# A two-layer encoder trunk on one core: order and waits in the odd layer's attention and output projection, in its router, and one step of the even layer

## The reference, cut to what matters

```
layer 0: h = x @ w_in -> heads A (sliding window, sinks, ALiBi) and B (forgetting attention)
         x = LN(ALPHA * x + concat(A, B) @ w_out);  x = LN(ALPHA * x + swiglu(x))
layer 1: h = x @ w_in -> q, k in two maps, v;  a = softmax(map 0) - lam * softmax(map 1)
         o = RMSNorm(a @ v) per head;              x = LN(ALPHA * x + o @ w_out)
         router: logits = x @ w_router, top 2 of 8, softmax gates
         x = LN(ALPHA * x + sum over the chosen experts of gate * swiglu_e(x))
```

## Time and profile before

| | us |
|---|---|
| median of 3 runs | 1427.79 |
| lowest, highest | 1424.65, 1428.18 |
| the profiled execution's own time | 1426.34 |
| its span, first to last instruction | 1424.6 |
| PE busy in the span | 1394.3 |
| DVE, ACT busy | 1126.4, 955.9 |
| mean granted clock of TensorE | 0.994 |

### The profile page before, as it was taken

How to read it: one execution, slowest core, us unless ns; L and a number is a source line. 1 busy time by engine, 2 the same in 40 slices (tenths; PEclk the granted TensorE clock), 3 DMA queues, 4 the chain that set the end, 5 groups by cost and what they waited for, 6 DMA issues and landing times.

```text
span 1424.6 us, 19267 instructions
## 1 busy us (share of the span) xinstructions
PE 1394.3 (98%) x7210; PEld 1182.1 (83%) x7210; DVE 1126.4 (79%) x1007; ACT 955.9 (67%) x880; POOL 36.8 (3%) x50
## 2 busy tenths in 40 slices
PE   8999999999999999999999999999999999999996
PEld 8998888889988888888888888888888888888874
DVE  4637655575567888888888888888888888889997
ACT  4655544545654777777777777777777777778774
POOL 1200000000001000000000000000000000000200
PEclk9999999999999999999999999999999999999998
DMA  9825555545146999999999999999999999999950
GB/s 365 324 81 207 203 182 186 198 148 178 60 179 253 424 422 421 412 391 375 366 383 379 375 399 374 372 390 385 374 365 386 382 372 401 376 377 366 384 248 31
DMA packets 64643, 444.85 MB, mean 312 GB/s; under 512 B 7416, under 2 KB 7440, under 8 KB 13008
## 3 DMA queue, kind: packets, MB, share of 16 engines
q1 hardware_dynamic: 59904, 425.75, 76.9%
q0 software_dynamic: 4544, 18.14, 3.5%
q10 hardware_dynamic: 144, 0.27, 0.1%
HBM read 431.54 MB, written 12.59 MB: 312 GB/s over the span
## 4 chain that ended last, share of the span: by engine, by line
PE 93%; DVE 4%; ACT 2%; DMA 1%; issue 0%; SPq 0%; DVEq 0%; ACTq 0%
PE ps L527 26%; PE ps L529 26%; PE ps L528 26%; PE ps L586 6%; PE ps L587 3%; PE ps L909 2%; DVE wlo L1292 1%; PE ps L647 1%; PE ps L699 1%; DMA raw<-w_dense 1%; ACT whi L1002 1%; PE ps L534 0%; PE ps L674 0%; PE ps L867 0%; PE ps L556 0%
## 5 line engine op out<-in xcount | busy, mean ns | idle before, releaser
L1292 DVE TENSOR_TENSOR wlo<-raw,whi 128x2048 fp32r<-128x2048 f32 x398 | 910.0, 2291 | 190.5 <-ACT whi L1002 189.4
L1002 ACT ACTIVATE whi<-raw 128x2048 fp32r<-128x2048 f32 x398 | 762.2, 1918 | 226.6 <-PE ps L529 224.5
L527 PE MATMUL ps<-whi,xt 128*128 128x512 f32 (+1 forms) x1144 | 442.1, 386 | 5.0 <-DVE wlo L1472 2.0
L529 PE MATMUL ps<-whi,xt 128*128 128x512 f32 (+1 forms) x1144 | 435.2, 380 | 0.0
L528 PE MATMUL ps<-wlo,xt 128*128 128x512 f32 (+1 forms) x1144 | 434.7, 380 | 0.0
L527 PEld LDWEIGHTS ps<-whi,xt 128*128 128x128 f32 x1144 | 216.1, 189 | 48.6 <-DVE wlo L1292 5.6
L529 PEld LDWEIGHTS ps<-whi,xt 128*128 128x128 f32 x1144 | 215.9, 189 | 41.1
L528 PEld LDWEIGHTS ps<-wlo,xt 128*128 128x128 f32 x1144 | 216.4, 189 | 38.2
L527 PE MATMUL ps<-whi,hth 128*128 128x512 f32 x464 | 181.8, 392 | 0.5 <-DVE wlo L1292 0.5
L529 PE MATMUL ps<-whi,htl 128*128 128x512 f32 x464 | 181.0, 390 | 0.0
L528 PE MATMUL ps<-wlo,hth 128*128 128x512 f32 x464 | 180.8, 390 | 0.0
(11 more groups left out here) (246 smaller groups left out, 843.9 us busy)
## 6 DMA issues: line engine op xcount, KB each, us to landing
raw<-w_moe SPq DMA_DIRECT2D x336, 1024.0 KB, 7.0
raw<-w_dense SPq DMA_DIRECT2D x62, 1024.0 KB, 4.8
x_slots<-hth POOLq DMA_DIRECT2D x16, 256.0 KB, 10.7
raw<-vec_rows POOLq DMA_DIRECT2D x4, 1024.0 KB, 7.2
y_rows<-work SPq DMA_DIRECT2D x8, 512.0 KB, 7.9
biasb<-x_slots POOLq DMA_DIRECT2D x7, 512.0 KB, 7.9
x<-x_in SPq DMA_DIRECT2D x2, 512.0 KB, 5.2
raw<-w_dense SPq DMA_DIRECT2D x2, 512.0 KB, 10.2
```

The costliest lines, as they stand in the source:

```text
L527: mm(o, lh, rh, start=start, stop=False)
L529: return mm(o, ll, rh, start=False, stop=stop)
L1002: A(unit(whi, j), raw[:, slot * UNIT:(slot + 1) * UNIT], ACT.Copy).then_inc(hi_rdy, 1)
L1292: dve.tensor_tensor(unit(wlo, j), raw[:, slot * UNIT:(slot + 1) * UNIT], unit(whi, j).bitcast(F32), ALU.subtract).then_inc(lo_rdy, 1)
```

## The change

It does the following.

- Layer 0: DVE's 16 bias instructions stand ahead of the split of unit 8 and no longer behind it.
- Turns go through the token tiles of one half of the heads before the other half. Values wait for the first half's copies, and for the rest only ahead of head 4.
- Layer 1: the scores of group 7 stand ahead of the turn of group 6 on PE and DVE; ACT keeps its order. Values 6 no longer wait for the last projection unit's copy at their start but ahead of head 6.
- The table load for the square root goes one unit earlier on ACT. Two warm-up matmuls ahead of `turn(4)` go away. The output projection starts after the first of the two tiles; unit 2 for block 1 is cut in halves around unit 3 for block 0.
- Router: positions of block 0 are taken inside block 1's logits, DVE makes block 0's one-hot at once, and PE gathers block 0's part of three of the four PSUM parts before it waits for block 1's choice. Two banks are cleared by matmuls with zeros. The warm-ups are 8, 4, 3, 8 for 8, 8, 4, 3, 8. On DVE the slot rows and a split stand behind the gather's subtractions.

The diff, cut to its core (new semaphores and the removed copies of blocks that only moved are left out):

```diff
-WARM_START, WARM_FIRST, WARM_NORM, WARM_HEADS = 9, 7, 12, 2
-WARM_ROUTE = (8, 8, 4, 3, 8)
+WARM_START, WARM_FIRST, WARM_NORM = 9, 7, 12
+WARM_ROUTE = (8, 4, 3, 8)
...
+        def part_bank(q):
+            return ps[(2, 3, 0, 1)[q]]
...
                 return i % 2, i // 2, (6, 7, 0, 1)[i]
+            if t == 5:
+                return i // 2, i % 2, i % 2
...
                    {4: [("scores", 4, 4)], 5: [("scores", 5, 0)], 8: [("scores", 6, 8)],
-                    9: [("turn", 6, 0), ("scores", 7, 0)],
-                    11: [("values", 6, 12), ("turn", 7, 0)]}]
+                    9: [("scores", 7, 0), ("turn", 6, 0)],
+                    11: [("values", 6, 11), ("turn", 7, 0)]}]
...
                         keep_warm(WARM_NORM, 3)
-                    if j == 0 and t == 4:
-                        keep_warm(WARM_HEADS, 4)
...
                 n = TR_BEFORE[g]
-                for kt in range(GROUPS[g][1] + 1):
-                    for half in range(2):
+                for half in range(2):
+                    for kt in range(GROUPS[g][1] + 1):
...
                         for i in range(4):
-                            r = pe.transpose(ps[prob_banks(g)[half]][:, i * P:(i + 1) * P],
+                            r = pe.transpose(ps[prob_banks(g)[n % 2]][:, i * P:(i + 1) * P],
...
                 kind, qblk, _ = GROUPS[g]
-                pe.wait_ge(pt_ev, TR_BEFORE[g + 1])
+                pe.wait_ge(pt_ev, TR_BEFORE[g] + qblk + 1)
...
                 for h in range(8):
+                    if h == 4:
+                        pe.wait_ge(pt_ev, TR_BEFORE[g + 1])
+                    if (g, h) == (6, 6):
+                        pe.wait_ge(in_ev, U_IN_E + U_IN_O)
...
-            def mix(k, tb, first, last, lh, ll):
+            def mix(k, tb, first, last, lh, ll, parts=range(4)):
                 h, l = as_rows(whi, k), as_rows(wlo, k)
-                for i in range(4):
+                for i in parts:
...
                         r.then_inc(y_left, 1)
-                if tb == 1:
+                if tb == 1 and parts[-1] == 3:
...
-            def out_rows(k0, u, tb):
+            def out_rows(k0, u, tb, parts=range(4)):
...
                     lambda r2, tb: xth[:, 2 * u + r2, tb * P:(tb + 1) * P],
-                    lambda r2, tb: xtl[:, 2 * u + r2, tb * P:(tb + 1) * P])
+                    lambda r2, tb: xtl[:, 2 * u + r2, tb * P:(tb + 1) * P], parts)
...
                 values(7)
-                turn(4, (0, 1))
+                turn(4, (0, 1), False)
+                turned(4, 0)
...
                 turn(4, (2, 3), False)
+                turned(4, 1)
                 turned(4, 3)
-                for u in range(3):
+                for u in range(2):
                     out_rows(k0, u, 1)
-                for tb in range(TB):
-                    out_rows(k0, 3, tb)
+                out_rows(k0, 2, 1, range(2))
+                out_rows(k0, 3, 0)
+                out_rows(k0, 2, 1, range(2, 4))
+                out_rows(k0, 3, 1)
...
+            chosen = rt[10]
+            def clear_part(q):
+                mm(part_bank(q)[:, 0:2 * P], y[:, 0:P], y[:, 0:2 * P], start=True, stop=False)
+            def gather_part(q, tb):
+                for kt in (2 * q + 1, 2 * q):
+                    first = q == 2 and tb == 0 and kt == 2 * q + 1
+                    c = slice(0 if first else (kt % 2) * P, (kt % 2) * P + P)
+                    r = mm(part_bank(q)[:, c], x[:, tb, kt * P:(kt + 1) * P],
+                           work[:, 1024 - P:1024 + P] if first else ohot[:, tb, :],
+                           start=first, stop=tb == TB - 1 and kt == 2 * q)
+                return r
+            def gather_last_part():
+                for kt in (6, 7):
+                    for tb in range(TB):
+                        r = mm(part_bank(3)[:, (kt % 2) * P:(kt % 2) * P + P], x[:, tb, kt * P:(kt + 1) * P],
+                               ohot[:, tb, :], start=tb == 0, stop=tb == TB - 1)
+                return r
...
                            start=kt == 0, stop=kt == KT - 1)
+                    if tb == 1 and kt == 3:
+                        pe.wait_ge(sel_rdy, 1)
+                        mm(ps[6][:, 0:8], tri, chosen[:, 0, :], start=True, stop=True).then_inc(pos0_ps, 1)
...
                         kt = 4 * half + i
-                        r = pe.transpose(ps[2 * tb + half][:, i * P:(i + 1) * P], x[:, tb, kt * P:(kt + 1) * P], ident)
+                        r = pe.transpose(ps[half][:, i * P:(i + 1) * P], x[:, tb, kt * P:(kt + 1) * P], ident)
...
             logits(0)
-            keep_warm(WARM_ROUTE[1], 3)
+            pe.wait_ge(ye_rdy, 1)
+            clear_part(0)
+            clear_part(1)
+            keep_warm(WARM_ROUTE[1], 1)
...
-            chosen = rt[10]
-            pe.wait_ge(sel_rdy, 1)
-            mm(ps[6][:, 0:8], tri, chosen[:, 0, :], start=True, stop=True)
-            mm(ps[6][:, 8:16], ones, chosen[:, 0, :], start=True, stop=False)
-            keep_warm(WARM_ROUTE[2], 7)
+            mm(ps[4][:, 256:264], ones, chosen[:, 0, :], start=True, stop=False)
+            pe.wait_ge(oh0_rdy, 1)
+            for q in range(3):
+                gather_part(q, 0)
             pe.wait_ge(sel_rdy, 2)
-            mm(ps[6][:, 8:16], tri, chosen[:, 1, :], start=False, stop=True).then_inc(pos_ps, 1)
+            mm(ps[4][:, 256:264], tri, chosen[:, 1, :], start=False, stop=True).then_inc(pos_ps, 1)
             mm(ps[7][0:1, 0:8], ones[:, 0:1], chosen[:, 1, :], start=False, stop=True).then_inc(cnt_ps, 1)
-            keep_warm(WARM_ROUTE[3], 5)
+            keep_warm(WARM_ROUTE[2], 5)
...
                 for q in range(4):
-                    for kt in range(2 * q, 2 * q + 2):
-                        for tb in range(TB):
-                            r = mm(ps[q][:, (kt % 2) * P:(kt % 2) * P + P], x[:, tb, kt * P:(kt + 1) * P],
-                                   ohot[:, tb, :], start=tb == 0, stop=tb == TB - 1)
+                    r = gather_part(q, 1) if q < 3 else gather_last_part()
...
             first_gather()
-            keep_warm(WARM_ROUTE[4], 5)
+            keep_warm(WARM_ROUTE[3], 5)
...
                     act.wait_ge(o_ps, min(g - 1, 4))
-                for kt in range(GROUPS[g][1] + 1):
-                    for half in range(2):
+                for half in range(2):
+                    for kt in range(GROUPS[g][1] + 1):
+                        if (g, half, kt) == (7, 0, 1):
+                            act.wait_ge(combined, 16)
                         act.wait_ge(tr_ps, n + 1)
-                        A(PT[g][:, kt, half * 512:(half + 1) * 512], ps[prob_banks(g)[half]][:, :],
+                        A(PT[g][:, kt, half * 512:(half + 1) * 512], ps[prob_banks(g)[n % 2]][:, :],
...
-                for what, g, _ in BETWEEN[layer].get(i, ()):
+                steps = BETWEEN[layer].get(i, ())
+                for what, g, _ in steps[::-1] if layer else steps:
...
                     even_end()
+                if k == K_OUT_O - 2:
+                    A(stats[:, 0, 5:6], eps[:, 0:1], ACT.Sqrt)
                 if k == K_OUT_O - 1:
-                    A(stats[:, 0, 5:6], eps[:, 0:1], ACT.Sqrt)
...
                     act.wait_ge(ga_ps, 1)
-                r = A(xth[:, 2 * q:2 * q + 2, 0:P], ps[q][:, 0:2 * P].rearrange("p (k n) -> p k n", k=2), ACT.Copy)
+                r = A(xth[:, 2 * q:2 * q + 2, 0:P], part_bank(q)[:, 0:2 * P].rearrange("p (k n) -> p k n", k=2), ACT.Copy)
...
                     norm(k, 2, 6, 5)
+                if k == 5:
+                    dve.wait_ge(cum_in, 16)
+                    for h in range(8):
+                        for b in range(TB):
+                            c = slice(P * b, P * b + P * (b + 1))
+                            r = dve.scalar_tensor_tensor(
+                                out=biasb[:, h, c], in0=cum_all[:, h, 0:P * (b + 1)],
+                                scalar=cumtok[:, b, h:h + 1], in1=bias[:, B_B + P * b:B_B + P * b + P * (b + 1)],
+                                op0=ALU.subtract, op1=ALU.subtract)
+                    r.then_inc(bb_rdy, 1)
+                    dve.wait_ge(bb_rdy, 1)
...
                     link(dve.tensor_copy(cumtok[:, :, :], ps[6][:, 0:16].rearrange("p (t n) -> p t n", t=TB)))
...
                                          in1=oh1[:, tb, :], op0=ALU.is_equal, op1=ALU.add).then_inc(sel_rdy, 1)
+                if tb == 0:
+                    dve.wait_ge(sel_rdy, 1)
+                    dve.wait_ge(pos0_ps, 1)
+                    link(dve.tensor_tensor(pos[:, 0, :], ps[6][:, 0:8], chosen[:, 0, :], ALU.mult))
+                    dve.tensor_scalar(ohot[:, 0, :], iota, 1.0, pos[:, 0, 0:1], ALU.add, ALU.is_equal).then_inc(oh0_rdy, 1)
...
             dve.wait_ge(pos_ps, 1)
-            link(dve.tensor_tensor(pos, ps[6][:, 0:16].rearrange("p (t n) -> p t n", t=TB), chosen, ALU.mult))
-            for tb in range(TB):
```

(38 more changed lines are left out.)

9 lines of the change are left out of this document (removed).

## The result

The changed kernel takes 1418.21 us (median; 1416.95 to 1421.11) against 1425.16 us for the kernel before (1424.63 to 1428.18): a ratio of 0.9948, 95% interval 0.9938 to 0.9958, or some 7 us less (medians of six executions each). The profiled execution took 1418.44 us with a span of 1416.7; before, 1426.34 and 1424.6.

The account below looks back on a forecast made before the run. TensorE, busy 98%, was taken to bound the kernel. Gains of 4.0 us before the router and 2.1 in it, less 0.2, gave 5.9 us; from two bases, the middle is 1421.2 us, range 1417 to 1426.

Parts of the forecast that it names:

- Bias: Layer 0, turn 1: bias ahead of the split lets ACT's copy start earlier, gain 1.0 us; 0.86 us of idle stays.
- Scores 7, values 6 and 7: Layer 1's attention: scores fill PE's waits, gain 1.5 us; finer waits of values 6 and 7 gain 0.7 us each.
- Head norm and table: Layer 1, block 0's turn: DVE's head norm is next late; with the table load moved, the shift there is 3.2 us.
- Waiting for one tile: Output projection: starts 0.65 us earlier, but the second turn's wait gives back all but 0.2; shift 3.4 us.
- Output order: Output projection: unit 3 is needed sooner and waits for its split, cost 0.4 us, bounds 0 to 0.6.
- Router: Logits to experts: dense gather replaces thin work and waits, low-clock stretch assumed half as long; gain 2.1 us.
- DVE's order: Ahead of the experts: moved slot rows and splits delay the fourth expert unit's split, cost 0.2 us (0 to 1).
- (a): Router: low clock lasts as long as before, edit worth 0.4 us, time 1422.1 to 1423.6 us; chance 0.18.
- (b): Router: no low clock, gain 7.3 us, time 1419 to 1420.5 us, or 1417 against another base; chance 0.10.
- (c): Layer 1: waits come back behind others; head norms move only 1 us, time 1425 us; chance 0.12.
- (d): Values 7 through router: clock falls and stays low some 45 us, slower, 1439 to 1441 us; chance 0.05.
- (e): Layer 1's attention: values 6 might still wait for ACT's late copy, 0.7 us missing; no chance given.

Follow-up runs that it names:

- e1: Kernel before with only the 16 bias instructions moved ahead of the split of unit 8; 1424.37 us, ratio 0.9984.
- e6: Kernel after with the finer waits of values 6 and 7 undone; one execution, 1420.26 us.
- e5: Kernel after with output unit 2's second block whole and unit 3 for both blocks behind it; one execution, 1416.89 us.
- e4: Kernel after with the square-root table load back behind the last projection unit on ACT; one execution, 1420.73 us.
- e9: Kernel before with 9 instead of 4 warm-up matmuls ahead of the wait for block 1's choice in the router; ratio 0.9997.
- e3: Kernel before with only the router's edits, DVE's new order included; 1423.78 us, ratio 0.9980.
- e8: Kernel after with router warm-ups of 0, 0, 0, 4 for 8, 4, 3, 8; ratio 0.9948, one execution of 7938.04 us left out.
- e10: Kernel after with router warm-ups of 0, 4, 3, 4 for 8, 4, 3, 8; 1417.12 us, ratio 0.9940.
- e7: Kernel after with DVE's slot rows and one split back ahead of the gather's subtractions; one execution, 1421.03 us.
- e11: Kernel after with e5's edit and router warm-ups of 8, 4, 3, 4 for 8, 4, 3, 8; 1419.26 us, ratio 0.9948.
- e12: Kernel after with e5's edit and router warm-ups of 0, 4, 3, 4 for 8, 4, 3, 8; 1419.92 us, ratio 0.9955.
- e2: Kernel before with only the edits of layer 1's attention, output order and table load; 1422.17 us, ratio 0.9973.

## Why the prediction was right, and where it was not

The forecast was 1421.2 us, the time 1418.21; faster, as forecast, and inside the range (1417 to 1426) near its lower end. PE's waits went where the sum had them; several terms were too small, one had the wrong sign, and the largest, the router's, came out by a low stretch whose length the traces don't tie to the edit.

**Bias:** 1.15 for 1.0. Right, shown by e1; of the 0.86 us of idle time that was to stay, 0.74 stayed.

**Scores 7, values 6 and 7:** 3.6 in sum (2.61 + 0.96) for 2.9. The mechanism was right and the sizes too small. Each wait was priced at its idle time; e6 shows 1.80 for two of 0.69, e5 0.60 for one of 0.31. Only for the two in front of turn 6 had I added a fill.

**Head norm and table:** at block 0's turn the shift is 3.7 for 3.2. That this chain would be late next was right (0.46 of wait); e4 prices the load at 1.0, as worked out; that two warm-ups less are worth up to 0.2 no run shows. Waiting for one tile gave 0.60 for 0.65, and the second turn took back 0.27 of a forecast 0.45.

**Output order:** a cost of 0.68 where I took 0.4, outside its bounds of 0 to 0.6. The wait (0.31) was where it was expected; its price was mis-sized in the same way. Arriving at the router, the change's part is 3.36 in layer 1 and 1.15 in layer 0, 4.5 for 4.0.

**Router:** 2.59 for 2.1 - 0.2. The low stretch is 3.41 us in place of 6.83, as assumed. But the reason that I gave is not borne out: e9 filled thin work and kept 6.83 us; the same old code has none at all in e1, and the new code has 3.41 us in e3, e5, e6, e8, e10 and the kernel after, but 6.83 in e4, e7, e11 and e12. With the warm-ups as in the change, six traces of the new code have 4.55 us in the mean, and the three of the old code (6.83, 6.83, 0) have 4.55 too. That the pair of profiles shows the halving is luck, as far as these traces go. Busy time by stretch, kernel e1, then e4 with its two low stretches:

```profile
449.00:452.00 3.00, 3.00 (x28) 3.00 (x27) 2.73 (x13) 1.34 (x4) 0.00 (x0) 1.00 1.00 421
...
437.50:440.70 3.20, 3.20 (x15) 3.02 (x14) 2.74 (x11) 0.00 (x0) 0.00 (x0) 0.50 0.41 150
444.30:447.50 3.20, 3.20 (x18) 2.95 (x17) 1.63 (x12) 2.81 (x3) 0.00 (x0) 0.50 1.02 430
```

At equal low time the edit is worth 1.0 us (e2's stage 21.33 and before's 21.45 against e4's 20.39, 6.8 us low in all). With none low there is only e1, 19.21 us; taking 1.5 us off the 18.86 of the kernel after for its low stretch (e4, with one more, has 20.39) gives about 17.3 (an estimate), worth 1.9. The other 0.7 to 1.6 us of the 2.59 belongs to the length of the low stretch in that execution. Whether the new code makes it short more often, the times don't settle either: the mean low time is less in e3 (15.9 us against 18.1 over the whole program) but also in e1 and e2 (15.4 and 16.1), whose router is the old one. The Trainium skill, TensorE: Matmul & The Clock Gate, "Part 1: The HAM clock gate", says that the phase varies from run to run; these traces agree, 0 to 6.83 us in one place of the same code.

**DVE's order:** the term that had the wrong sign. I priced what the moved slot rows would cost in their new place (0.2; the trace has no wait there: the split for the fourth unit runs from 455.07 and ends at 457.36, before PE needs it) and not what they would have cost in the old one. e7 shows 0.8 us of PE idle and 0.9 to 1.0 in the stage.

**Base and end:** 1.50 us of the profiled difference is the start of the program, 1.20 of it the place of a low stretch. 0.7 is given back behind the router, half over the experts and half in the tail, for which no one wait stands out. Between the two medians, 1425.16 and 1418.21, the difference is 6.95 us; the sum was 5.9. So of the 3.0 us by which the forecast missed, 1.9 is the base: with more runs the median of before is 1425.16, and the same sum from it gives 1419.3. Of the other 1.1 the table explains 0.5 (0.5 ahead of the router and 0.7 in it, less 0.7 given back); the rest is inside the scatter of two medians of six runs. The clock has a part in that scatter: the mean low time of the six executions after is 14.6 us, that of the 30 of the kernel before beside e1 is 18.1, and at the price found for one low stretch (1.5 us for 3.41) the difference is worth some 1.5 us, an estimate.

**Rivals:** (a), a low clock as long as before, was not seen in the kernel after but was in e4 (20.39 us of stage) and costs 1.5; the edit is then worth 1.0 and not 0.4. (b), none, was not seen with the new code. (c) and (d) are refuted by the table above and the 98%: no wait of the head norm takes the gain, and the clock did not stay low in any trace. That the clock held after 1.62 us of idle, the argument against (d), was luck: e9 has a fall there, of 3.41 us. (e): values 6 does not wait.

## What to carry to other kernels

On the engine that bounds a kernel a short wait costs its idle time and more, here 0.2 to 0.3 us more for each, so waits of 0.3 to 0.7 us are worth filling with independent work. A step moved on another engine has to be priced in its old place in the new schedule too, not in its new one alone; and warm-up matmuls that stand in the queue are work on the path, so they are tried smaller as soon as the wait that they cover shrinks, over several executions and not by one trace. Read small differences between executions of like granted clock, since one low stretch more or less is worth as much as a whole edit.

## What the runs showed of the hardware

Falls of the clock after short idle times, in some executions only. Kernel e2 has one in layer 0, 0.9 us after the end of its 1.90 us of waiting in turn 1 (busy time by stretch), and e9, above, one after 1.62 us ahead of the projection; the profile of before has the same two idle times and neither fall. Over all 14 traces each of the two waits stands in four and has a fall behind it in one; where the waits are shorter (0.75 and 1.02 us, ten traces each) none has.

```profile
66.20:69.50 3.30, 3.30 (x18) 3.30 (x17) 2.07 (x3) 1.00 (x2) 0.00 (x0) 0.50 0.54 168
```

One such stretch of 3.41 us at 1.2 GHz costs about 1.5 us (stage of e4 against that of the kernel after, 20.39 and 18.86). An edit that takes away an idle time may therefore save more than the wait now and then; e1's mean over its runs is 2.0 us below that of before for a wait shortened by 1.15, which fits but was not shown to have this cause. And one matmul instruction of 128 columns took 0.12 us at the full clock and 0.23 at the low one while it stood in a row of its kind (16 in 1.95 us; in the gather from 441.17, 12 in 3.23 us, of which two have twice the columns).
